# Streaming-encoder block with product-key experts: seven early units of the first expert table, the second table wholly by list, gate groups closer together, 86 rows gathered ahead

## The reference, cut to what matters

```python
x = x + jnp.concatenate([y_a, y_b], axis=-1) @ w_o
h = rmsnorm(x, g_ffn)
qr = (h @ w_pq).reshape(b, t, 8, 2, 128)
sc = einsum('bthpd,hpnd->bthpn', qr, sub_keys)
...
expert = i0 * 128 + i1                # (b, t, 8, 16)
g = jax.nn.softmax(c_top, axis=-1)
a = gelu(einsum('bthkd,btd->bthk', u_tab[expert], h))
x = x + einsum('bthk,bthkd->btd', g * a, v_tab[expert])
```

## Time and profile before

| what | value |
|---|---|
| median of 3 runs | 1521.25 us (1520.91 to 1523.61) |
| the profiled execution | 1521.85 us |
| its span | 1519.8 us |
| PE busy | 1451.8 us, 96% of the span |
| DVE busy | 1154.4 us, 76% |
| ACT busy | 487.8 us, 32% |
| POOL busy | 430.5 us, 28% |
| moved by DMA | 516.25 MB, mean 340 GB/s |
| of that POOL's queue q0 | 294.93 MB, 49.0% of 16 engines |
| SP's q1 and ACT's q10 | 154.09 MB, 27.9%, and 66.35 MB, 10.6% |

### The profile page before, as it was taken

One profiled execution on the slowest core, in us unless ns is written; L12 is line 12 of the kernel. 1 busy time (PEld: TensorE's weight loads), 2 busy tenths in 40 slices (PEclk: granted clock), 3 DMA queues, 4 the chain that ended last, 5 costly groups with the idle time before them and its releaser, 6 DMA issues.

```text
span 1519.8 us, 21779 instructions
## 1 busy us (share of the span) xinstructions
PE 1451.8 (96%) x7977; PEld 1099.0 (72%) x7977; DVE 1154.4 (76%) x1797; ACT 487.8 (32%) x1402; POOL 430.5 (28%) x422
## 2 busy tenths in 40 slices
PE   8999999999999999999989999998897899999998
PEld 6767888888899999999989999983333343444443
DVE  5425688586687799999377777778766899998997
ACT  6646656764655200000134444457000000000000
POOL 2020000000001232222210111126444666665762
PEclk9999999999999999999999999999989999999999
DMA  9764544637669899999999999999999999999997
GB/s 348 277 139 111 163 134 139 206 131 240 205 232 407 335 398 422 421 422 421 422 421 421 422 422 416 403 414 417 419 416 417 404 392 398 398 412 352 382 408 281
DMA packets 115528, 516.25 MB, mean 340 GB/s; under 512 B 26112, under 2 KB 28288, under 8 KB 63312
## 3 DMA queue, kind: packets, MB, share of 16 engines
q0 software_dynamic: 57776, 294.93, 49.0%
q1 hardware_dynamic: 47888, 154.09, 27.9%
q10 hardware_dynamic: 9792, 66.35, 10.6%
HBM read 628.91 MB, written 3.41 MB: 416 GB/s over the span
## 4 chain that ended last, share of the span: by engine, by line
PE 53%; DMA 23%; DVE 16%; issue 4%; POOL 3%; ACT 1%; another core or an unknown queue 0%; POOLq 0%; ACTq 0%; SPq 0%; DVEq 0%
PE ps L1643 12%; PE ps L1597 12%; DMA acts<-in_v_tab,acts 8%; PE ps L1379 6%; PE ps L1384 6%; PE ps L1381 6%; DMA late<-in_u_rows,sel 6%; DVE late L1192 3%; DMA raw<-in_v_tab,acts 3%; DMA late<-in_v_tab,acts 3%; DVE ps L1201 2%; PE ps L1401 2%; PE ps L1543 2%; PE ps L1539 2%; PE ps L1538 2%
## 5 line engine op out<-in xcount | busy, mean ns | idle before, releaser
L877 DVE TENSOR_TENSOR w_lo<-raw,w_hi 128x512 fp32r<-128x512 f32 (+1 forms) x288 | 188.1, 682 | 129.7 <-ACT w_hi L570 127.7
L1597 PE MATMUL ps<-acts,late 128*128 128x128 f32 x1984 | 233.4, 277 | 7.3 <-DMA late<-in_u_tab 6.0
L1597 PEld LDWEIGHTS ps<-acts,late 128*128 128x128 f32 x1984 | 227.6, 193 | 10.8 <-ACT acts L783 5.7
L1597 PE MATMUL ps<-acts,raw 128*128 128x128 f32 x1952 | 228.7, 276 | 5.3 <-DMA raw<-in_u_tab 3.7
L1597 PEld LDWEIGHTS ps<-acts,raw 128*128 128x128 f32 x1952 | 222.1, 192 | 9.0 <-DMA raw<-in_u_tab 4.4
L570 ACT ACTIVATE w_hi<-raw 128x512 fp32r<-128x512 f32 (+1 forms) x288 | 170.2, 622 | 85.3 <-PE ps L1543 40.3
L1643 PE MATMUL ps<-raw,acts 128*128 128x512 f32 x352 | 161.8, 611 | 13.1 <-DMA raw<-in_v_tab,acts 10.7
L1643 PE MATMUL ps<-acts 128*128 128x512 f32 x336 | 156.9, 618 | 16.7 <-DMA acts<-in_v_tab,acts 15.5
L1201 DVE SCALAR_TENSOR_TENSOR ps<-acts,sel,ps 128x2048 f32<-128x2048 f32 x63 | 148.4, 2355 | 16.8 <-DMA acts<-in_v_tab,acts 9.4
L1201 DVE SCALAR_TENSOR_TENSOR ps<-late,sel,ps 128x2048 f32<-128x2048 f32 x63 | 148.4, 2355 | 15.2 <-DMA late<-in_v_tab,acts 7.9
L1643 PE MATMUL ps<-late,acts 128*128 128x512 f32 x336 | 150.3, 597 | 9.8 <-DMA late<-in_v_tab,acts 8.5
(11 more groups left out here) (225 smaller groups left out, 1958.0 us busy)
## 6 DMA issues: line engine op xcount, KB each, us to landing
raw<-in_w_in SPq DMA_DIRECT2D x72, 512.0 KB, 4.2
late<-in_u_tab SPq DMA_DIRECT2D x32, 1024.0 KB
raw<-in_u_tab SPq DMA_DIRECT2D x31, 1024.0 KB
raw<-in_u_tab ACTq DMA_DIRECT2D x30, 1024.0 KB
late<-in_u_tab ACTq DMA_DIRECT2D x30, 1024.0 KB
raw<-in_w_o SPq DMA_DIRECT2D x32, 512.0 KB, 4.3
raw<-in_w_pq SPq DMA_DIRECT2D x32, 512.0 KB, 4.7
acts<-in_u_tab SPq DMA_DIRECT2D x5, 1024.0 KB, 8.8
```

Of the source, the lines that this page charges most:

```text
L877: V.tensor_tensor(wlo[slot_no][:, 0:w], raw[j % NRAW][:, half * w:half * w + w], whi[slot_no][:, 0:w].bitcast(F32), ALU.subtract).then_inc ...
L1597: ins = mm(ps[:, q, 0:N_DN], unit[:, k * P:k * P + P], hF[:, k, :], start=k == 0, stop=k == KD - 1)
```

## The change

- **Early units.** Seven units instead of five are loaded ahead. Unit 0 goes out on SP between the halves of `w_o`, after a wait for the attention products (`y_mm`); units 1 to 4 after each four loads of the second half, unit 5 after two of the eight rounds of four `w_pq` loads, unit 6 after six. For this the loops over `w_o` are written out, `x2n` moves to another region, and the buffer of queries shrinks from 16 to 4 slots, with a wait of ACT for the scores (`score_mm`) that read a slot before it is written again. The first ring loads are units 8, 9, 7 and 10.
- **The fill of ones.** POOL waits for seven units before it, not for five.
- **The second table by list.** Units 0 to 5 are gathered by POOL as the others are. Their list needs activations that are final, so it is made before the end of the first table, and the gate groups are put closer together: five groups in nine units instead of one in two, the last at unit 121 instead of 126.
- **Rows.** 86 instead of 88 are asked for ahead of the first list unit, four more among units 1 to 5, and the remaining 166 at 1.35 for each unit instead of 168 at 1.40. The last two rows are asked for after the last unit.
- PE's gate stage is written out instead of a loop.

```diff
-    NRING, NROW = 4, 8
+    NRING, NROW, N_FIRST = 4, 8, 7
...
-    V_FULL = 6
+    V_RING = 6
...
-        A_QR = TT * D
-        qr = region(A_QR, 16 * SEQ).rearrange("p (c t) -> p c t", c=16)
+        x2n = [region(A_HF + D * b, D) for b in range(TT)]
+        qr = [early[:, 256:512], early[:, 1024:1280], early[:, 1408:1664], gate_low[:, 0:SEQ]]
...
-        first_units = [region(2 * UNIT * i, 2 * UNIT) for i in (0, 1, 4, 7, 5)]
+        first_units = [region(2 * UNIT * i, 2 * UNIT) for i in (0, 1, 2, 3, 4, 7, 5)]
...
-        ROWS_U = 88
+        ROWS_U = 86
...
-        UNIT_GROUPS = [(V_FULL, 22), (22, 64), (64, NKEY)]
+        UNIT_GROUPS = [(0, V_RING), (V_RING, 22), (22, 64), (64, NKEY)]
 
         def group_chunk(g):
 
             if g < 2:
                 return FIRST_G + 2 + g
-            return FIRST_G + 2 * g
+            return FIRST_G + 4 + 9 * ((g - 2) // 5) + 2 * ((g - 2) % 5)
+
+        GROUP_AT = {group_chunk(g): g for g in range(N_GRP)}
+        LISTED_AT = group_chunk(N_GRP - 1) + 2
...
             for group in range(2):
-                with sp.Fori(0, D // 512) as n:
+                if group:
+                    sp.wait_ge(y_mm, 16)
+                    first_unit(0)
+                for n in range(D // 512):
                     for j in range(4):
                         k = 8 * group + 2 * j
-                        load(n * 4 + (B_WO + 16 * group + j), j, wo[:, k:k + 2, ds(n * 512, 512)])
-            def u_unit(v):
-                return io["u_tab"][ds(v * P, P), :]
+                        load(n * 4 + (B_WO + 16 * group + j), j, wo[:, k:k + 2, n * 512:n * 512 + 512])
+                    if group:
+                        first_unit(1 + n)
             def query_weights(first, end):
                 with sp.Fori(first, end) as i:
                     for j in range(4):
                         load(i * 4 + (B_PQ + j), j, io["w_pq"][ds(i * (4 * P) + j * P, P), :])
-            def first_unit(j):
-                sp.dma_start(first_units[j], u_unit(j)).then_inc(first_in[j], 16)
-
-            query_weights(0, 3)
...
+            query_weights(0, 2)
+            first_unit(5)
+            query_weights(2, 6)
             sp.wait_ge(x2_stored, 16)
             sp.wait_ge(xT_mm, KD)
-            first_unit(4)
-            query_weights(7, 8)
-
-            sp.wait_ge(lo_done, 2 * (B_U + 3) - 2 * (NRAW - 1))
-            sp.dma_start(ring[1], u_unit(NRING + 1)).then_inc(unit_in[1], 16)
+            first_unit(6)
+            query_weights(6, 8)
+
+            for j in range(2):
+                sp.wait_ge(lo_done, 2 * (B_U + 2 * j + 1) - 2 * (NRAW - 1))
+                sp.dma_start(ring[j], u_unit(2 * NRING + j)).then_inc(unit_in[j], 16)
...
-            def v_unit(u):
-                sp.dma_start(ring[u], io["v_tab"][u * P:u * P + P, :]).then_inc(unit_in[u], 16)
-            for u in (0, 2):
-                sp.wait_ge(unit_used, NKEY + u + 1 - NRING)
-                v_unit(u)
-            sp.wait_ge(unit_used, NKEY)
-            v_unit(4)
-            sp.wait_ge(hs_moved, 4)
-            sp.wait_ge(row_used, ROWS_SB)
-            v_unit(5)
...
-            pool.wait_ge(unit_used, NRING + 1)
+            pool.wait_ge(unit_used, N_FIRST)
             pool.memset(region(A_ONES, NKEY * N_DN - A_ONES), 1.0).then_inc(ones_set, 1)
             gathers(R_FRONT + 6, ROWS_U)
             done = ROWS_U
-            for u in range(V_FULL, NKEY):
+            for u in range(NKEY):
                 for k, (first, end) in enumerate(UNIT_GROUPS):
                     if u == first:
                         pool.wait_ge(unit_ready, k + 1)
-                pool.wait_ge(unit_used, NKEY + u + 1 - V_FULL)
-                pool.indirect_dma_start(ring[u % V_FULL], None, io["v_tab"], bass.IndirectOffsetOnAxis(ap=unit_rows[:, u:u + 1], axis=0),
-                                        bounds_check=LAST_ROW, oob_is_err=False).then_inc(value_in[u % V_FULL], 16)
-                end = ROWS_U + (len(ROWS) - ROWS_U) * (u + 1 - V_FULL) // (NKEY - 2 - V_FULL)
+                if u < NRING:
+                    pool.wait_ge(unit_used, NKEY + u + 1 - NRING)
+                elif u == NRING:
+                    pool.wait_ge(unit_used, NKEY)
+                elif u == NRING + 1:
+                    pool.wait_ge(hs_moved, 4)
+                    pool.wait_ge(row_used, ROWS_SB)
+                else:
+                    pool.wait_ge(unit_used, NKEY + u + 1 - V_RING)
+                pool.indirect_dma_start(ring[u % V_RING], None, io["v_tab"], bass.IndirectOffsetOnAxis(ap=unit_rows[:, u:u + 1], axis=0),
+                                        bounds_check=LAST_ROW, oob_is_err=False).then_inc(value_in[u % V_RING], 16)
+                end = ROWS_U + max(u - 1, 0) if u < V_RING else ROWS_U + V_RING - 2 + (len(ROWS) - ROWS_U - V_RING + 2) * (u + 1 - V_RING) // (NKEY + 1 - V_RING)
...
+                if c >= 4:
+                    act.wait_ge(score_mm, TT * (c // 2 - 1))
+                nc.scalar.activation(qr[c % 4], ps[:, c % 2, 0:SEQ], ACT.Copy).then_inc(qr_done, 1)
...
-                if c % 2 and c > 3:
+                if c % 2 and N_FIRST <= c < NKEY - NRING:
...
+                if c == LISTED_AT:
+                    act.wait_ge(gated, N_GRP)
+                    units_used(*UNIT_GROUPS[0])
...
+                if c in GROUP_AT and GROUP_AT[c] + 1 < N_GRP:
+                    hots(GROUP_AT[c] + 1)
+                apply(c - 1)
+                if c - 1 in GROUP_AT and GROUP_AT[c - 1] >= 2:
                     next_row()
                     gate(g)
                     g += 1
+                if c == LISTED_AT + 1:
+                    list_units(0)
+                if c > LISTED_AT and (NKEY - 1 - c) % 2 == 0:
+                    next_row()
...
+            for c in range(FIRST_G, NKEY):
+                u_chunk(c // NRING, c % NRING)
+                if c in GROUP_AT:
+                    gate_group(GROUP_AT[c], GROUP_AT[c] % 2, GROUP_AT[c] < 2)
```

More of the change, by code:

```diff
@@ L814, in odd_unit, with units_used @@
                 act.wait_ge(unit_used, c + 1 - NRING)
-                src = io["u_tab"] if c < NKEY else io["v_tab"]
-                act.dma_start(ring[c % NRING], src[c % NKEY * P:c % NKEY * P + P, :]).then_inc(unit_in[c % NRING], 16)
+                act.dma_start(ring[c % NRING], io["u_tab"][c * P:c * P + P, :]).then_inc(unit_in[c % NRING], 16)
+            def units_used(first, end):
+                for u in range(first, end):
+                    if u >= 12:
+                        act.wait_ge(used_done, u - 11)
+                    at = P * (u % 12)
+                    nc.scalar.activation(early[:, at:at + P], acts_c[u], ACT.Abs, accum_out=used_sum[:, u:u + 1]).then_inc(used_done, 1)
             for c in range(NKEY):
                 gelu(c)
-                if c % 2 and c > 3:
+                if c % 2 and N_FIRST <= c < NKEY - NRING:
                     odd_unit(c + NRING)
@@ L831, in _ @@
                         row_gelu(h)
-            def units_used(first, end):
-                for u in range(first, end):
-                    if u >= V_FULL + 12:
-                        act.wait_ge(used_done, u - V_FULL - 11)
-                    at = P * (u % 12)
-                    nc.scalar.activation(early[:, at:at + P], acts_c[u], ACT.Abs, accum_out=used_sum[:, u:u + 1]).then_inc(used_done, 1)
+                if c == LISTED_AT:
+                    act.wait_ge(gated, N_GRP)
+                    units_used(*UNIT_GROUPS[0])
             act.wait_ge(gelu_done, NKEY)
@@ L844, in _ @@
             act.wait_ge(applied, NKEY - FIRST_G)
-            act.wait_ge(gated, N_GRP)
-            for first, end in UNIT_GROUPS:
+            for first, end in UNIT_GROUPS[1:]:
                 units_used(first, end)
@@ L1215, in list_units @@
                 dve.wait_ge(expert_in, 16)
-                dve.wait_ge(used_done, end - V_FULL)
+                dve.wait_ge(used_done, end)
                 link(V.tensor_scalar(used_sum[:, first:end], used_sum[:, first:end], 0.0, SKIP, ALU.is_equal, ALU.mult))
@@ L1623, in _ @@
             slot_transposes()
[L1624 to L1632 removed]
+            for c in range(FIRST_G, NKEY):
+                u_chunk(c // NRING, c % NRING)
+                if c in GROUP_AT:
+                    gate_group(GROUP_AT[c], GROUP_AT[c] % 2, GROUP_AT[c] < 2)
             pe.wait_ge(gated, N_GRP)
             def v_chunk(i, q, first=False, last=False):
[L1638 to L1641 removed]
+                pe.wait_ge(value_in[q], i * 16 + 16)
                 for n in range(KD // 4):
[L1643 removed]
+                    ins = mm(out_bank(n), acts_c[i * V_RING + q], ring[q][:, 512 * n:512 * n + 512], start=first, stop=last)
                     if last:
@@ L1650, in _ @@
             pe.wait_ge(applied, NKEY - FIRST_G)
-            for q in range(1, V_FULL):
+            for q in range(1, V_RING):
                 v_chunk(0, q)
-            for i in range(1, NKEY // V_FULL):
-                for q in range(V_FULL):
```

(6 more changed lines are left out.)

62 lines of the change are left out of this document (16 added, 46 removed).

## The result

The changed kernel takes 1524.09 us (median of 19 runs, 1523.29 to 1525.72); the kernel before took 1521.25 beside it (19 runs). The ratio is 1.0017, with an interval of 1.0011 to 1.0024. So the change costs 2.8 us: less than the 0.2% of the forecast's bound, but on the other side of zero from the forecast 1516.5.

What follows compares the result with a forecast made beforehand. It took the second half as bound by DMA bytes first, PE and DVE as tight late, and row gathers as binding in the first-table stage. Terms: 0.7 + 3 - 6.5 + 0 + 0.5 - 2.5 = -4.8, 1516.5 us; range 1508 to 1527.

Steps and rivals of the forecast that it cites:

- Early units in w_o: Loads of w_o's second half: unit 0 delays the next load, units 1 to 4 cost nothing; +0.7 us, ends 0 and +2.5.
- What the two more units buy: First table's start: nothing gained directly, about 10 us DMA idle, fill and next gather 7.1 us later; +3 us.
- Six units by list: Second table's first six units: each skips 0.454 MB, 1.1 us of DMA time; -6.5 us, ends -7.5 and -4.
- Gate groups closer: End of first table: 32 groups as before, ACT about fits a neighbouring pair; 0, ends -1 and +2 us.
- Start of the second table: First list unit on POOL's queue behind about three rows, landing 9.1 us after asking; +0.5 us, ends 0 and +7.
- row 89: Second table's start on POOL: the wait for the 82nd used row was taken as covered by queued work; 0.
- 86 rows, 1.35 a unit: Second table: 4 rows fewer ahead when unit 125 is asked for; -2.5 us, ends -5.7 and +3.
- the queue moves the wait to PE: Rival: 7.1 us come out at unit 66, PE starts the second table 5 us late; +6.3, 1527.5 us, chance 0.17.
- The saved bytes are given back: Rival: PE and DVE set the pace from 1216 us on, the tail gives +1; -0.3, 1521 us, chance 0.26.
- The lists skip little: Rival: the lists of the second table's first six units bring no gain; +1.7, 1523 us, chance 0.03.

Runs made afterwards that it cites:

- e2: Changed kernel, but POOL asks for rows 14 to 23 ahead of its wait for seven units and the fill of ones: 1518.35 us, ratio 0.9975.
- e7: Changed kernel, but five early units instead of seven, loaded between the w_pq loads, POOL waiting for five: 1521.81 us, ratio 0.9998.
- e11: Kernel of e5, but units 0 to 5 of the second table loaded whole by SP: 1518.45 us, ratio 0.9974.
- e5: Changed kernel with the edits of e2 and e3 together: 1512.78 us, ratio 0.9943.
- e8: Kernel of e4, but gate groups spread over every second unit up to unit 126: 1525.95 us, ratio 1.0028.
- e3: Changed kernel, but 89 rows ahead of the first list unit, one behind each of units 1 to 5, DVE working one in each of units 123 to 127: 1519.29 us.
- e4: Changed kernel, but units 0 to 5 of the second table loaded whole by SP, not gathered by list on POOL: 1525.70 us, ratio 1.0024.
- e1: Changed kernel, but rows among the list units at 1.38 a unit instead of 1.35, the last asked for before unit 126: 1524.38 us, ratio 1.0011.
- e9: Kernel of e5, but up to three rows more asked for ahead of list units 42 to 85, given back by unit 125: 1512.62 us, ratio 0.9934.

## Why the prediction was wrong

*Early units in w_o*, +0.7: small, as forecast. The gelu of unit 0 came 0.4 us later; over all thirteen profiles it starts between 516.6 and 520.2, so no more than that can be said.

*What the two more units buy*, +3 from ends of 0 and +7.1: **near its size, but by luck**. The mechanism was forecast to the number: the gather near 543, some 10 us idle (9.7 measured, 11.0 less 1.3). But the price was put on two rows of DMA time, less 2 us won back, as if part of the idle time were free. It is paid: taking half of it away (e2) gave 5.7 us. Against that stands what the units buy, put at "nothing directly": they take bytes out of the stretch after 510 (2.86 MB, e7). The two errors cancel. This term and the one above were 3.7 us in the sum, and e7 measures 2.3.

*Six units by list*, -6.5: about right where the rest lets it show (e11 against e5, 5.7 us); the bytes saved were 0.56 MB a unit, not 0.454 (the 0.595 MB of the earlier trace rows are a mean over units and rows).

*Gate groups closer*, 0: right (e8, 0.3 us). They moved PE's time, which looked like a loss at unit 126, and gave it back.

*Start of the second table*, +0.5 from ends of 0 and +7: **the step that failed**. It asked when the first list unit lands, and for PE. PE found it there at 1023.49 without a wait. What it left out is POOL's stand of 9.86 us in front of that unit, with few rows on its queue and SP and ACT out of units: 6.5 us idle in 1000 to 1060, 0 before. Filling it gave 4.8 us (e3). The prediction counted rows *ahead* of the unit as a cost; there were too few. It did ask whether POOL's queue lasts through a wait, but only at row 89: "its queue has work to go on with, so I take that wait as covered: 0". At unit 0 the queue had not. Because of it the lists, with their start, gave 1.6 us (e4) where the sum had 6.0.

*86 rows, 1.35 a unit*, -2.5: **the second, smaller miss**. Taking the ratio back cost 0.3 us (e1), too little to tell from nothing: DVE's last row stayed where it was. That 86 rows go ahead instead of 88 has no run of its own.

By the runs that take single parts back, the early units cost 2.3 us instead of 3.7 (e7), lists and start gave 1.6 instead of 6.0 (e4), the groups 0.3 instead of 0 (e8) and the ratio 0.3 instead of 2.5 (e1). That is +0.1 us, where the sum had -4.8 and the result was +2.8. So 4.9 of the 7.6 us by which the forecast was off are found, 4.4 of them at the start of the second table; what the other 2.7 us are stays open, and each of these differences is uncertain by a microsecond or two.

Of the rivals, *the queue moves the wait to PE* had the right sign and the wrong engine: PE waited less at the first gate group and not at all for the first list unit. *The saved bytes are given back* had its sign at the tail, DVE ending after PE, and a time within 3.1 us. That PE and DVE take no earlier data from 1216 on is refuted by e2, e3 and e5, where both took 4 to 11 us of it in full; that idle DMA time is hardly paid there, as the account suggests, is on its side. *The lists skip little* has the nearest number, 1523, by luck: the six lists skipped more than was taken, not less.

## What to carry to other kernels

Where a stage is bound by transfers, sum idle time of the DMA engines and bytes, not delays of instructions: in e3 PE's second table started 11.6 us later than in the kernel before, and the kernel was 2.6 us faster, while the gaps in the queues at 530 and 1015 cost about their length (e2, e3). Where the engines run at their pace, as after 1216, idle DMA time looks to be free. Ask of each wait that is put into an issuing engine's stream what is still on the queues while it stands, above all where several queues become one and where bytes have just been moved ahead. A transfer moved into an earlier, idle stage pays only if the work that it made room for is ready to be asked for: here 2.86 MB were moved ahead of 510 us, and the early units still cost 2.3 us.

## What the runs showed of the hardware

DVE and PE at 96% and 97% of their own pace in 1216 to 1420 (80 rows by 2.46 us and 466 records by 0.426 us, of 204 us) did not keep the kernel from taking earlier data: with data 11 us earlier both ended 11 us earlier (e5). Idle DMA time was paid at 510 to 545 (4.9 us gone, 5.7 us won, e2) and at the seam (3.8 us gone, 4.8 us won, e3); 4.1 us more of it in e9 than in e5, 2.3 of them after 1216, changed the median by 0.2 us.
